# First head pair's rows written twice to DRAM by the Pool queue; two steps moved across a barrier

## What is computed

```python
q_n, k_c, v_c, k_s, v_s, k_w, v_w, gates, q_f, k_f, v_f, logf = project(h, w_in, ...)   # 1024 tokens, heads of 64
kc, vc, c_end, ovl, ksb, vsb = nsa_full_keys(k_c, v_c, k_s, v_s, ...)
lc = einsum(qg, kc) * scale + bias      # compressed keys, 8 query heads over 2 key heads
ls = einsum(qg, ks_sel) * scale + bias  # selected blocks
lw = einsum(qg, kw) * scale + bias      # sliding window
lf = einsum(q_f, k_f) * scale + decay   # FoX, 8 heads, causal
```

## Time and profile before

| | |
|---|---|
| median of 3 runs | 1880.42 us (1878.41 to 1886.46) |
| the profiled execution's own time | 1885.07 us |
| its span in the trace | 1883.3 us |
| PE matmul busy | 1758.1 us (93%) |
| DVE, ACT, Pool busy | 1037.7, 690.6, 254.0 us (55%, 37%, 13%) |
| DMA | 206.34 MB, mean 110 GB/s |

### The profile page before, as it was taken

One profiled execution on the slowest core, in us unless ns is written; L12 is line 12 of the kernel. 1 busy time (PEld: TensorE's weight loads), 2 busy tenths in 40 slices (PEclk: granted clock), 3 DMA queues, 4 the chain that ended last, 5 costly groups with the idle time before them and its releaser, 6 DMA issues. The chain is left out here.

```text
span 1883.3 us, 35725 instructions
## 1 busy us (share of the span) xinstructions
PE 1758.1 (93%) x13749; PEld 1556.0 (83%) x13749; DVE 1037.7 (55%) x1987; ACT 690.6 (37%) x1363; POOL 254.0 (13%) x565
## 2 busy tenths in 40 slices
PE   7889999799895999999998999999999999999998
PEld 6879999776563666666675879999999999999998
DVE  4433333123362676767766558676566665665665
ACT  4201001221331566555666553133333332344343
POOL 3000006320401213223222000000000000000000
PEclk9989999989997999999998999999999999999999
DMA  4433956644999404040200223123222224331112
GB/s 132 174 94 115 230 158 125 181 143 162 301 329 244 102 2 102 1 102 2 91 1 35 74 103 110 48 79 112 82 69 82 78 69 150 132 123 59 46 40 104
DMA packets 143984, 206.34 MB, mean 110 GB/s; under 512 B 23689, under 2 KB 101944, under 8 KB 143762
## 3 DMA queue, kind: packets, MB, share of 16 engines
q1 hardware_dynamic: 113938, 143.37, 24.8%
q0 software_dynamic: 16480, 52.41, 9.2%
q10 hardware_dynamic: 13408, 8.42, 2.1%
HBM read 163.11 MB, written 45.20 MB: 111 GB/s over the span
## 5 line engine op out<-in xcount | busy, mean ns | idle before, releaser
L2016 ACT ACTIVATE probs<-psum,neg_max 128x640 f32<-128x640 f32 (+7 forms) x192 | 137.9, 718 | 117.9 <-DVE neg_max L2153 113.2
L183 PE MATMUL psum<-x_hi,w_hi 128*128 128x352 f32 x528 | 173.0, 328 | 8.0 <-DVE w_lo L631 3.4
L183 PE MATMUL psum<-h_parts,down_hi 128*128 128x352 f32 x528 | 171.8, 325 | 6.0 <-DVE h_parts L3132 4.3
L184 PE MATMUL psum<-x_lo,w_hi 128*128 128x352 f32 x528 | 172.5, 327 | 0.0
L185 PE MATMUL psum<-x_hi,w_lo 128*128 128x352 f32 x528 | 172.3, 326 | 0.0
L184 PE MATMUL psum<-h_parts,down_hi 128*128 128x352 f32 x528 | 170.7, 323 | 0.0
L185 PE MATMUL psum<-h_parts,down_lo 128*128 128x352 f32 x528 | 170.7, 323 | 0.0
L183 PE MATMUL psum<-hf_hi,op_hi 128*128 128x264 f32 x576 | 163.7, 284 | 0.6 <-DVE silu L3113 0.6
L185 PE MATMUL psum<-hf_hi,op_lo 128*128 128x264 f32 x576 | 163.8, 284 | 0.0
L184 PE MATMUL psum<-hf_lo,op_hi 128*128 128x264 f32 x576 | 163.6, 284 | 0.0
L1938 PE MATMUL psum<-ident,probs 128*128 128x128 f32 x848 | 141.5, 292 | 6.6 <-ACT probsT L2026 5.1
(11 more groups left out here) (432 smaller groups left out, 4173.8 us busy)
## 6 DMA issues: line engine op xcount, KB each, us to landing
fox_ring<-in_cache_fox_kv SPq DMA_DIRECT2D x128, 256.0 KB, 5.8
zT<-z_stage SPq DMA_DIRECT2D x22, 528.0 KB, 2.9
w_ring<-in_w_in POOLq DMA_DIRECT2D x22, 512.0 KB, 5.4
down_ring<-in_w_ffn_down SPq DMA_DIRECT2D x44, 256.0 KB, 2.6
raw<-in_w_ffn_gate SPq DMA_DIRECT2D x9, 1024.0 KB, 7.8
raw<-in_w_ffn_up SPq DMA_DIRECT2D x9, 1024.0 KB, 5.4
h_dram<-stage POOLq DMA_DIRECT2D x8, 1056.0 KB, 6.0
nsa_page<-in_cache_nsa_kv POOLq DMA_DIRECT2D x64, 128.0 KB, 6.2
```

Of the source, the lines that this page charges most:

```text
L183: nc.tensor.matmul(dst, w_hi, x_hi, start=start, stop=False, skip_group_check=onto)
L184: nc.tensor.matmul(dst, w_hi, x_lo, start=False, stop=False, skip_group_check=onto)
L2016: nc.scalar.activation(probs[:, u % 4, 0:n], slot_of(u), ACT.Exp, bias=neg_max[:, u % 4:u % 4 + 1], scale=1.0, accum_out=denom[:, m % 2, a ...
```

## The change

Pool copies five tiles of `zT` (the first pair's NSA queries, the selected keys, the window keys, the first pair's fox queries and fox keys; columns 0 to 1023) to a new DRAM tensor `z2`, each twice, with ten DRAM-to-DRAM DMAs of 512 KB. They stand in its stream of B behind a new wait for the prompt chunk's load. In `z2` a tile lies as (head, copy, row, token), so that one load, read as "(copy row) head token", fills all 128 partitions of a tensor that was loaded in halves. SP's loads of pair 0's queries, the selected and the window keys become one load of 1 MB each. The fox loads of pair 0 become two loads of 1 MB and the unchanged rest, and move from B's stream to the head of C's. Pool's sixteen spreading copies move from the end of B to the head of its stream in C. The waits' counts follow.

```diff
+DOUBLED = {"q_nsa": TILE["q_n"], "k_slc": TILE["nsa_kv"] + 2, "k_win": TILE["win_kv"], "q_fox": TILE["q_f"], "k_fox": TILE["fox_kv"]}
+def doubled(env, name):
+    return env["z2"][list(DOUBLED).index(name)].rearrange("e c d t -> (c d) e t")
...
+        z2 = nc.dram_tensor("z2", (len(DOUBLED), 2, 2, DH, T), F32).ap()
...
                 load_tables(sp, env, c)
-                load_queries(sp, env, 0, env["kv_loaded"])
+                sp.wait_ge(env["z2_stored"], 32 * len(DOUBLED))
+                sp.dma_start(env["q_nsa"][:, 1], doubled(env, "q_nsa")).then_inc(env["kv_loaded"], 16)
...
                 load_shared(sp, env, nsa_kv_prompt)
-                PE.wait(sp, ("use_v", RN - 1, 3))
-                load_fox_keys(sp, env, 0, env["fox_loaded"][0])
-                load_fox_rest(sp, env, fox_kv_prompt, 0)
...
+                pool.wait_ge(chunk_loaded[0], CT_LOADED[4])
+                for n, tile in enumerate(DOUBLED.values()):
+                    for copy in range(2):
+                        pool.dma_start(env["z2"][n, :, copy], zT[tile].rearrange("(e d) n -> e d n", d=DH)[:, :, 0:T]).then_inc(env["z2_stored"], 16)
                 read_four(1)
...
-                pool.wait_ge(filled, 5)
-                for e in range(2):
-                    expand(nc.gpsimd, env["bias_cmp"], env["bias_cx"], e).then_inc(env["first_table"], 1)
...
-    for half in range(2):
-        part = slice(half * DH, (half + 1) * DH)
-        sp.dma_start(env["k_slc"][part, :, :], rows[(TILE["nsa_kv"] + 2) * P:(TILE["nsa_kv"] + 3) * P, 0:T].rearrange("(g d) t -> d g t", g=G)).then_inc(done, 16)
-        sp.dma_start(env["k_win"][part, :, :], rows[TILE["win_kv"] * P:(TILE["win_kv"] + 1) * P, 0:T].rearrange("(g d) t -> d g t", g=G)).then_inc(done, 16)
+    for name in ("k_slc", "k_win"):
+        sp.dma_start(env[name][:, :, :], doubled(env, name)).then_inc(done, 16)
...
 def fox_loads(hp):
-    return 176 * (hp // 2 + 1)
+    return 176 * (hp // 2 + 1) - (0 if hp % 2 else 96)
...
             @block.sync
             def _(sp):
+                for name in ("q_fox", "k_fox"):
+                    sp.dma_start(low[name][:, 0], doubled(env, name)).then_inc(fox_loaded[0], 16)
+                load_fox_rest(sp, env, fox_kv_prompt, 0)
                 sp.wait_ge(env["nsa_out_stored"], NSA_OUT * RN)
...
-                                pe.wait_ge(kv_loaded, 224)
+                                pe.wait_ge(kv_loaded, 144)
...
                 pool.wait_ge(filled, 5)
+                for e in range(2):
+                    expand(nc.gpsimd, bias_cmp, bias_cx, e).then_inc(env["first_table"], 1)
```

More of the change, by code:

```diff
@@ L142, in program @@
         kv_loaded = sem("c_kv_loaded")
+        z2_stored = sem("b_z2_stored")
         with ExitStack() as early:
@@ L1732, in load_shared @@
 def load_shared(sp, env, nsa_kv_prompt):
-    rows = env["zT"].rearrange("n p t -> (n p) t")
     done = env["kv_loaded"]
-    for half in range(2):
-        part = slice(half * DH, (half + 1) * DH)
-        sp.dma_start(env["k_slc"][part, :, :], rows[(TILE["nsa_kv"] + 2) * P:(TILE["nsa_kv"] + 3) * P, 0:T].rearrange("(g d) t -> d g t", g=G)).then_inc(done, 16)
-        sp.dma_start(env["k_win"][part, :, :], rows[TILE["win_kv"] * P:(TILE["win_kv"] + 1) * P, 0:T].rearrange("(g d) t -> d g t", g=G)).then_inc(done, 16)
+    for name in ("k_slc", "k_win"):
+        sp.dma_start(env[name][:, :, :], doubled(env, name)).then_inc(done, 16)
     sp.dma_start(env["v_slc"].rearrange("p t g d -> p t (g d)"), nsa_kv_prompt[0, 0, :, 3].rearrange("(t p) g d -> p t (g d)", p=P)).then_inc(done, 16)
```

## The result

Timed side by side, 13 executions of each kernel: before 1881.2 us median, the changed kernel 1870.22 (1864.65 to 1877.52), ratio 0.9943 with a 95% interval of 0.9929 to 0.9957. That is 10.7 us less (8.1 to 13.4), where 9.6 were forecast.

The account below looks back on a forecast made before the run. PE, busy 93%, was taken as bound, with a 13.7 us hole before C held by SP at the barrier. PE starting C at 591.2 instead of 600.77 saves 9.6 us: 1870.8 us, eight times in ten 1865.5 to 1878.

Parts of the forecast that it names:

- What bounds: PE's 13.7 us hole before stage C's first scores: `v_win` lands at about 597.0, the last 3.7 us are the barrier's.
- Part 1: Fox rows behind the barrier: SP's queueing goes, alone PE starts at 597.0 instead of 600.8; barrier then at 589.5 earliest.
- Part 2: One load instead of halves: 362 instead of 214 GB/s, three shared tensors 6.0 us earlier (4.6 to 6.5), `v_win` at 591.1.
- Part 4: Pool's spreading copies at the head of stage C: 2.88 us, hidden; under 1 us if PE could start at 589.5.
- Part 3: Ten DRAM copies from about 406 to 436 or 450: nothing, covered by a DMA hole of some 60 us; uncovered 29 us.
- Part 5: Fox loads at stage C's head: values land at 604.2, PE wants them at 604.8; covered by 0.6 us.
- rival B: Fox rows at stage C's head become the bound, slipping 2 to 5 us: gain 4 to 8, 1872 to 1876; chance 0.11.
- Clock: PE's granted clock, 0.50 from 600 to 618 after the hole: no gain counted from the shorter hole, at most 3 us.
- C: Rival: width changes nothing, 214 GB/s belongs to reading `zT`, not to 64 partitions; gain 0.5 us, 1880; chance 0.06.
- D: Rival: ten copies pile up on two DMA engines, stage B's ring refills come 24 us late; 1895; chance 0.07.
- E: Rival: PE's clock comes back early in stage C, besides the forecast gain: 12 to 14 us less, 1867; chance 0.10.

Follow-up runs that it names:

- experiment 7: Changed kernel without the ten copies, its wide loads reading two neighbouring `zT` tiles (other rows than the reference's): 1871.28 us, ratio to before 0.9946.
- 6: Kernel before plus only the ten copies and SP's wait for them, nothing reading the copies: 1880.51 us, ratio to before 0.9994.

## Why the prediction was right, and where only its sum was

The sum, 9.6 us, was measured as 9.6 at the place and 10.7 (8.1 to 13.4) in the time. Its terms were not all right: one term was counted that was worth nothing, one that was worth about as much was not counted, and that the two were of one size is luck.

**What bounds, and Part 1: failed.** "`v_win`'s bytes are in at 596.0 ... landed at about 597.0, and the last 3.7 us of the hole are the barrier's alone." It landed at 600.6, and the moves alone gave 1.0000. The step that failed is the reading of a landing from the mean rate of all engines: the wait ends with the last increment. The lag of 1 us came from a single load of one MB at 206 GB/s; in the four traces with the shared loads in halves the last four increments are spread over 3.1 to 4.7 us, and that is what was missing.

"After it the barrier is held by the latest other engine: ACT's store issue" is true of the changed kernel (the barrier opens 3.2 us behind the start of PE's last work, forecast 3.1), but only because the spreading copies moved as well, a step to which the prediction gave no price. With them in B on Pool C begins 5.5 us later. Pool's end was read from its last busy row; its drain, in no view, ends 4.7 us behind it.

**Part 2: right in kind, its size wrong.** 214 to 362 GB/s were forecast, 220 to 335 measured: 3.15 MB take 14.3 and 9.4 us at these rates, 4.9 instead of 6.0. The landing moved by 30.1 - 20.5 = 9.6, because the lag shrank too: the last four increments lie within 0.3 us in after (up to 2.0 in the other kernels with wide shared loads) against 4.0. These two make 8.6 of the 9.6, by my estimate; the last microsecond I can't assign. So the wide loads carry the term that Part 1 claimed for the barrier, and the sum came out. Whether it is the 64 partitions or the number of loads that makes the lag, no run parts.

**Part 4: a term of its own that was costed at nothing.** The prediction asked only who waits for the copies behind the barrier, and there it was right: nobody. It did not ask what they hold in front of it. Width alone 4.2 us of C's start (30.3 to 26.1), with the spreading moved 8.4, with the fox rows moved too 9.6 (9.3 by the changed kernel's second profile), of which the last step is within the scatter of the landings. The moves alone, with the loads in halves, are worth nothing.

**Part 3: right.** No cost with the cover; PE waits for no ring slot. Without cover it was put at 29 us; it measured 16, by another path.

**Part 5: right, but thinner than said.** Forecast: the fox values land 13.1 us behind C's start, wanted at 13.7. Measured 13.6 (599.0 against 585.38), 0.15 ahead of the first fox scores. In the second profile it is 14.3, and a landing releases the fox scores, which the prediction names as the sign of rival B. It is B to the extent of 0.6 us.

**Clock: right.** It is 0.50 (1.2 GHz) at C's start in both kernels. From C's first matmul on it stays there for 18.3 us in before and for 19.6 in the changed kernel (20.1 in its second profile), so the shorter hole brings it back no earlier. In the changed one:

```profile
590.00:600.00 10.00, 5.79 (x28) 4.32 (x30) 6.50 (x24) 3.32 (x12) 0.86 (x2) 0.50 1.06 301
```

**The rivals.** C fell with experiment 7 (`zT` read at 348 GB/s), D with 6 and 7. E, the clock coming back early, fell with these numbers too. What is left of the hole is 3.6 us between the starts of PE's last work and of C's first; PE's last work itself, DVE's copy, ACT's store and its drain fill 2.9 of it (581.76 to 584.71), the barrier 0.2, and the landing at 585.2 stands just behind. The version with DVE's copies came out the same within the interval.

## What to carry to other kernels

Parts of a change can be worth nothing alone and be needed together: here three things ended within 5 us of each other (a landing at 600.6, SP at 600.2, Pool's drain at 596.2). The wide loads brought the first two forward, and only then did Pool's drain show. So when a wait goes, list every engine's end and the last increment of every load, not only the one that the wait names. And compare profiles by distances between shared events: the spans differed by 20 us, the kernels by 10.

## What the runs showed of the hardware

- **Pool's drain at a stage's end** lasts 6.77 us in all four kernels that have the spreading copies at the end of B on Pool (6.770 to 6.777 in five traces); 2.1 us of it pass while the copies still run, 4.7 behind them. It lasts 8.0 to 9.9 us where a DMA issue is Pool's last act of B, 10.9 to 12.5 us at the end of the first stage, 17.4 to 18.1 at the end of D's stream; and 0.57 us at the end of C, the one stage in which Pool issues no DMA at all though it computes to the end. DVE's, ACT's and PE's are at most 1.5 us at the ends of the first stage, B and C. That it belongs to the DMAs which Pool has issued in the stage fits all of these, but no run takes those away; it is not shown. Giving the copies to DVE opens the barrier 4.2 us behind the start of PE's last work instead of 10.
- **The last increments of a group of loads can trail.** The wait on `kv_loaded` ends with two loads into 128 partitions in every kernel. Where the loads ahead of them go into 64, the last four increments are spread over 3.1 to 4.7 us in four executions; where the large ones are wide, over 0.3 to 2.0 in nine. It is no rule for all such loads: on `fox_loaded`, before C's first fox scores, the same spread is 0.8 to 3.6 us in five executions with halves and 0.4 to 2.2 in eight without. The cause stays open, and the records don't name the DMA engine. The Trainium skill, "DMA: Bandwidth & Descriptors", section "Latency and other measured facts", says that two of the sixteen are usually slower in traces, but ties this to descriptors made in software. These loads stand in SP's hardware queue, so it doesn't explain them.
- **Copies from DRAM to DRAM** went as 10400 packets for 5.28 MB. Their mean of 508 bytes misleads: the trace's packets are 1280 of 4096 bytes, one for each row of each copy, and 9120 of 4 bytes. The page's counts above say nearly the same (some 8940 more packets under 512 bytes than in before, 1280 more between 2 and 8 KB). What the small ones carry, no view says. Ten copies in a row kept all engines busy. Pool's queue from 400 to 445 us (packets, MB, share of the 16 engines' time):

```profile
q0 software_dynamic: 10400, 5.28, 42.8%
```
